# Two query blocks per round in the local attention of a four-layer fp32 kernel

## The reference

```
o = for each 128-query block i, each head h:
    s = q_i k[i-1..i] * scale + (-slope_h * distance, or -1e30 outside the 128-token window)
    m = max(max(s), sink_h);  p = exp(s - m)
    denom = sum(p) + exp(sink_h - m)
    o = (p / denom) v[i-1..i]
x = x + o @ w_out          # q, k are RMS-normed per head first
```

## Time and profile before

| | |
|---|---|
| median of 3 runs | 2162.7 us (2161.97 to 2165.08) |
| profiled execution: time, span | 2161.92 us, 2159.9 us |
| busy in the span | PE 2033.6 (94%), DVE 1127.4 (52%), ACT 796.0 (37%), POOL 136.7 (6%) |
| granted TensorE clock, mean | 0.972 of full |
| local attention stage with its fills | about 665 to 785 us from the span's start |

### The profile page before, as it was taken

The page is one execution under the profiler, slowest core; times in us unless marked ns, Lnnn a source line. Parts: engine busy times, 40 slices in busy tenths (PEclk is TensorE's granted clock), DMA queues, the critical chain, the costliest instruction groups (busy, mean ns, idle before and its releaser), DMA issues. The chain is left out here.

```text
span 2159.9 us, 25160 instructions
## 1 busy us (share of the span) xinstructions
PE 2033.6 (94%) x9068; PEld 1575.3 (73%) x9068; DVE 1127.4 (52%) x1730; ACT 796.0 (37%) x1243; POOL 136.7 (6%) x115
## 2 busy tenths in 40 slices
PE   7967999999999999999999898799989999999999
PEld 5834788888776667888877676588845577888887
DVE  4367456445446756653563765833334536553553
ACT  3145334223335644432342343411145534431341
POOL 0020200000021010000001002200021110000000
PEclk9978999999999999999999999899979999999999
DMA  5200232232221112223222231132200112223222
GB/s 188 95 4 1 78 116 88 88 108 90 82 100 60 40 59 78 97 88 107 98 68 98 78 100 64 54 117 97 87 15 30 44 61 78 96 93 106 94 75 100
DMA packets 30523, 173.85 MB, mean 80 GB/s; under 512 B 3392, under 2 KB 3520, under 8 KB 15472
## 3 DMA queue, kind: packets, MB, share of 16 engines
q1 hardware_dynamic: 30304, 172.66, 23.2%
q10 hardware_dynamic: 144, 0.21, 0.0%
HBM read 170.66 MB, written 2.20 MB: 80 GB/s over the span
## 5 line engine op out<-in xcount | busy, mean ns | idle before, releaser
L539 PE MATMUL banks<-xn_hi,w_hi 128*128 128x512 f32 x1672 | 659.3, 394 | 32.4 <-ACT xn_hi L1047 16.6
L539 PE MATMUL banks<-xn_hi,w_lo 128*128 128x512 f32 x1672 | 654.8, 392 | 0.0
L539 PE MATMUL banks<-xn_lo,w_hi 128*128 128x512 f32 x1672 | 649.0, 392 | 1.1 <-DVEq L1473 1.1
L994 ACT ACTIVATE w_hi<-raw 128x2048 fp32r<-128x2048 f32 (+2 forms) x156 | 271.7, 1742 | 396.1 <-PE banks L539 392.2
L1391 DVE TENSOR_TENSOR w_lo<-raw,w_hi 128x2048 fp32r<-128x2048 f32 (+3 forms) x162 | 339.9, 2098 | 130.7 <-ACT w_hi L994 109.6
L539 PEld LDWEIGHTS banks<-xn_hi,w_hi 128*128 128x128 f32 x1672 | 316.7, 189 | 107.7 <-issue 24.2
L539 PEld LDWEIGHTS banks<-xn_lo,w_hi 128*128 128x128 f32 x1672 | 315.9, 189 | 70.1 <-DVEq L1473 3.4
L539 PEld LDWEIGHTS banks<-xn_hi,w_lo 128*128 128x128 f32 x1672 | 317.0, 190 | 66.4 <-issue 0.2
L1488 DVE SCALAR_TENSOR_TENSOR tmp<-banks,par,tmp 128x511 f32<-128x511 f32 x132 | 98.4, 745 | 269.4 <-ACT tmp L1072 269.4
L1072 ACT ACTIVATE tmp<-banks,par 128x512 f32<-128x512 f32 x132 | 95.6, 775 | 357.3 <-PE banks L539 357.3
L539 PE MATMUL banks<-hid_hi,w_hi 128*128 128x512 f32 x528 | 207.3, 393 | 3.1 <-DVE w_lo L1391 3.1
(11 more groups left out here) (222 smaller groups left out, 2033.5 us busy)
## 6 DMA issues: line engine op xcount, KB each, us to landing
raw<-weights SPq DMA_DIRECT2D x117, 1024.0 KB, 4.8
raw<-weights SPq DMA_DIRECT2D x24, 768.0 KB, 4.2
raw<-weights SPq DMA_DIRECT2D x24, 640.0 KB, 3.7
att<-scratch SPq DMA_DIRECT2D x32, 256.0 KB, 3.1
x<-xt SPq DMA_DIRECT2D x4, 512.0 KB, 5.8
out<-x SPq DMA_DIRECT2D x4, 512.0 KB, 4.0
raw<-weights SPq DMA_DIRECT2D x2, 512.0 KB, 3.4
con<-consts SPq DMA_DIRECT2D x1, 864.0 KB, 12.6
```

Of the source, the lines that this page charges most:

```text
L539: return pe.matmul(psum[:, 2 * p + m, :], w[:, at_:at_ + P], chunk(x_part, k), start=start, stop=stop)
L994: act.activation(w_hi[:, sl], raw[:, sl], ACT.Identity).then_inc(hi_done, 1)
```

## The change

The loop runs over rounds of two steps, g = 0, 2, ... 34. TensorE does the scores of two steps, the fills of two, the turns of the two steps before, and the values of the two before those. ScalarE and VectorE wait for both steps of a round (`g | 1`) before they read a bank, since two steps now share each bank of scores and of transposes, 256 columns each (`c_half`). `c_prob` becomes eight tiles of 257 columns, `c_slot` halves of four chunks, and the bias tiles move. ScalarE's order is `high` at g % 4 == 0, exps of two steps, copies of two steps, `norm_job` at g % 4 == 2, and `hi_piece`. VectorE's is `finish` of two, `maxima` of two, `output` and both `alibi` at g % 4 == 0, `evacuate` of units done in the round before, `lo_piece`, and `scaled` at g % 4 == 2. TensorE's `norm_job` stands at g % 4 == 0, between turns and values. No arithmetic is added or removed.

```diff
         def c_slot(m, g):
-            return att[:, (12 + 2 * (g % 2) + m) * T:(13 + 2 * (g % 2) + m) * T]
+            return chunk(att, 12 + 2 * (g // 2 % 2) + m, 256 * (g % 2), 256 * (g % 2) + 256)
         def c_prob(m, g):
-            return chunk(att, 8 + 2 * (g % 2) + m)
+            at_ = 7 * T + 257 * (2 * (g % 4) + m)
+            return att[:, at_:at_ + 257]
+        def c_half(m, bank, g, w):
+            return psum[:, bank + m, 256 * (g % 2):256 * (g % 2) + w]
...
                 def scores(g):
-                    if g:
-                        pe.wait_ge(c_max, 2 * g)
+                    if g >= 2:
+                        pe.wait_ge(c_max, 2 * (g - g % 2))
...
                 def turn(g):
-                        if g:
-                            pe.wait_ge(c_copied, 2 * g - 1 + m)
+                        if g >= 2:
+                            pe.wait_ge(c_copied, 2 * (g - g % 2) - 1 + m)
...
-                for g in range(C_STEPS + 2):
+                for g in range(0, C_STEPS + 4, 2):
                     if g < C_STEPS:
                         scores(g)
-                    fill(g)
-                    if 1 <= g <= C_STEPS:
+                        scores(g + 1)
+                    if g < C_STEPS + 2:
+                        fill(g)
+                        fill(g + 1)
+                    if 2 <= g <= C_STEPS:
+                        turn(g - 2)
                         turn(g - 1)
-                    if g >= 2:
-                        values(g - 2)
-                    if g % 4 == 1 and g // 4 + 1 < C_PAIRS:
+                    if g % 4 == 0 and g // 4 + 1 < C_PAIRS:
                         norm_job(2 + g // 4 + 1)
+                    if g >= 4:
+                        values(g - 4)
+                        values(g - 3)
...
                 def copy(g):
-                        act.wait_ge(c_pt, 2 * g + m + 1)
+                        act.wait_ge(c_pt, 2 * (g | 1) + m + 1)
...
-                for g in range(C_STEPS + 2):
-                    if g % 4 == 2 and g > 4:
-                        high(g // 4 - 1)
+                for g in range(0, C_STEPS + 4, 2):
+                    if g % 4 == 0 and g > 4:
+                        high(g // 4 - 2)
                     if g < C_STEPS:
                         exps(g)
-                    if 1 <= g <= C_STEPS:
+                        exps(g + 1)
+                    if 2 <= g <= C_STEPS:
+                        copy(g - 2)
                         copy(g - 1)
                     if g % 4 == 2 and g // 4 + 1 < C_PAIRS:
                         norm_job(2 + g // 4 + 1)
                     for s, g0, n in C_FILL:
-                        if g0 <= g < g0 + 2:
-                            hi_piece(s + 1, g - g0, 2)
+                        for q in range(2):
+                            if g <= g0 + q < g + 2:
+                                hi_piece(s + 1, q, 2)
...
                 def maxima(g):
-                    if g >= 2:
-                        dve.wait_ge(c_pt, 2 * g - 2)
+                    if g >= 4:
+                        dve.wait_ge(c_pt, 2 * g - 6)
                     for m in range(2):
-                        dve.wait_ge(c_scored, 2 * g + m + 1)
+                        dve.wait_ge(c_scored, 2 * (g | 1) + m + 1)
...
-                for g in range(C_STEPS + 2):
-                    if 1 <= g <= C_STEPS:
+                for g in range(0, C_STEPS + 4, 2):
+                    if 2 <= g <= C_STEPS:
+                        finish(g - 2)
                         finish(g - 1)
                     if g % 4 == 0 and 0 < g < C_STEPS:
                         sink_columns(g // 4)
                     if g < C_STEPS:
                         maxima(g)
-                    if g % 4 == 2 and g > 4:
-                        output(g // 4 - 1)
-                    if g % 4 < 2 and g // 4 + 1 < C_PAIRS:
-                        alibi(g // 4 + 1, g % 4)
+                        maxima(g + 1)
+                    if g % 4 == 0 and g > 4:
+                        output(g // 4 - 2)
+                    if g % 4 == 0 and g // 4 + 1 < C_PAIRS:
+                        alibi(g // 4 + 1, 0)
+                        alibi(g // 4 + 1, 1)
                     for s, m, done in C_UNIT_STEPS:
-                        if done == g - 1 and done >= 0 and (s, m) != (q + 1, 0):
+                        if g - 2 <= done < g and done >= 0 and (s, m) != (q + 1, 0):
                             evacuate(s, m)
                     for s, g0, n in C_FILL:
-                        if g0 + 1 <= g < g0 + 3:
-                            lo_piece(s + 1, g - g0 - 1, 2)
-                    if g % 4 == 3 and g // 4 + 1 < C_PAIRS:
+                        for part in range(2):
+                            if g <= g0 + 1 + part < g + 2:
+                                lo_piece(s + 1, part, 2)
+                    if g % 4 == 2 and g // 4 + 1 < C_PAIRS:
                         scaled(2 + g // 4 + 1)
```

More of the change, by code:

```diff
@@ L312, in c_slot @@
         def c_slot(m, g):
-            return att[:, (12 + 2 * (g % 2) + m) * T:(13 + 2 * (g % 2) + m) * T]
+            return chunk(att, 12 + 2 * (g // 2 % 2) + m, 256 * (g % 2), 256 * (g % 2) + 256)
         def c_prob(m, g):
-            return chunk(att, 8 + 2 * (g % 2) + m)
+            at_ = 7 * T + 257 * (2 * (g % 4) + m)
+            return att[:, at_:at_ + 257]
+        def c_half(m, bank, g, w):
+            return psum[:, bank + m, 256 * (g % 2):256 * (g % 2) + w]
+        c_bias = [chunk(att, 5), chunk(att, 6)]
         def c_width(g):
@@ L864, in scores @@
                         h = 64 * m
-                        pe.matmul(psum[:, 4 + m, 0:w], qn[it % 2][h:h + 64, i * P:(i + 1) * P], kn[it // 4][h:h + 64, lo:lo + w],
+                        pe.matmul(c_half(m, 4, g, w), qn[it % 2][h:h + 64, i * P:(i + 1) * P], kn[it // 4][h:h + 64, lo:lo + w],
                                   start=True, stop=True).then_inc(c_scored, 1)
@@ L871, in turn @@
                         pe.wait_ge(c_fin, 2 * g + m + 1)
-                        if g:
-                            pe.wait_ge(c_copied, 2 * g - 1 + m)
+                        if g >= 2:
+                            pe.wait_ge(c_copied, 2 * (g - g % 2) - 1 + m)
                         for j in range(w // P):
-                            last = pe.transpose(psum[:, 6 + m, j * P:(j + 1) * P], c_prob(m, g)[:, 256 - w + j * P:256 - w + (j + 1) * P], ident)
+                            last = pe.transpose(c_half(m, 6, g, w)[:, j * P:(j + 1) * P], c_prob(m, g)[:, 256 - w + j * P:256 - w + (j + 1) * P], ident)
                         last.then_inc(c_pt, 1)
@@ L1216, in copy @@
                     for m in range(2):
-                        act.wait_ge(c_pt, 2 * g + m + 1)
-                        if m == 0 and g >= 2:
-                            act.wait_ge(c_pv, g - 1)
-                        act.activation(c_slot(m, g)[:, 0:w], psum[:, 6 + m, 0:w], ACT.Identity).then_inc(c_copied, 1)
+                        act.wait_ge(c_pt, 2 * (g | 1) + m + 1)
+                        if m == 0 and g >= 4:
+                            act.wait_ge(c_pv, g - 3)
+                        act.activation(c_slot(m, g)[:, 0:w], c_half(m, 6, g, w), ACT.Identity).then_inc(c_copied, 1)
                 def high(it):
@@ L1676, in alibi @@
                 def alibi(it, m):
-                    me.mark(dve.tensor_scalar(bias[it % 2][:, 256 * m:256 * m + 256], ccol("window", 0, 256),
+                    me.mark(dve.tensor_scalar(c_bias[it % 2][:, 256 * m:256 * m + 256], ccol("window", 0, 256),
                                               ccol("c_slope", 2 * it + m), None, ALU.mult))
                 def sink_columns(it):
-                    at_ = att[:, 8 * T:12 * T].rearrange("p (a b t) -> p a b t", a=2, b=2)[:, :, :, 256:257]
-                    of = neg_sink[:, 2 * it:2 * it + 2].rearrange("p (o b t) -> p o b t", o=1, t=1).to_broadcast([P, 2, 2, 1])
+                    at_ = att[:, 7 * T:7 * T + 8 * 257].rearrange("p (a b t) -> p a b t", a=4, b=2)[:, :, :, 256:257]
+                    of = neg_sink[:, 2 * it:2 * it + 2].rearrange("p (o b t) -> p o b t", o=1, t=1).to_broadcast([P, 4, 2, 1])
                     me.mark(dve.tensor_copy(at_, of))
@@ L1689, in maxima @@
                         me.wait()
-                    if g >= 2:
-                        dve.wait_ge(c_pt, 2 * g - 2)
+                    if g >= 4:
+                        dve.wait_ge(c_pt, 2 * g - 6)
                     for m in range(2):
                         n = 2 * (g % 4) + m
-                        dve.wait_ge(c_scored, 2 * g + m + 1)
+                        dve.wait_ge(c_scored, 2 * (g | 1) + m + 1)
                         dve.tensor_tensor_reduce(
-                            out=c_prob(m, g)[:, 256 - w:256], in0=psum[:, 4 + m, 0:w],
-                            in1=bias[it % 2][:, 256 * m + 256 - w:256 * m + 256], scale=-1.0,
+                            out=c_prob(m, g)[:, 256 - w:256], in0=c_half(m, 4, g, w),
```

(19 more changed lines are left out.)

## The result

| | before | after |
|---|---|---|
| median, 4 runs each | 2162.8 us | 2197.4 us (2196.8 to 2198.7) |
| ratio, 95% interval | | 1.0159 (1.0141 to 1.0177) |
| span of the profiled execution | 2159.9 us | 2196.2 us |
| PE busy in the span | 2033.6 | 2041.6 (93%) |

The changed kernel is 34.6 us slower; forecast were 29 us. Two executions among all runs of this document that took far longer than the others of their kernel (4127.7 us of the kernel before, 2914.8 us of the version "with one order mended") are left out of the comparisons. The lines have moved: scores are now L872, fills L825, turns L882, values L897, the norm job L861, `scaled` L1688, `evacuate` L1675 and L1679, `lo_piece` L1664, `hi_piece` L1201.

The account below looks back on a forecast made before the run. TensorE, busy 94% of the span, was taken to bound the kernel. Steps 0 to 27 at +23.8 and the rest at -1.3 made +22.5; with +7 for clock, 2161.9 became 2191.4, stated as 2191.5 us, range 2168 to 2207.

Parts of the forecast that it names:

- rival 1: Stalls in the attention stage as the forecast summed them: 2180 to 2203 us, chance 70%.
- its signs: Scores and fills released late, granted clock under 0.9 in 740 to 800, stage about 150; wrong if idle under 10 us.
- The norm chain: Round B's norm job stands behind four exponentials and copies: next scores at 8.0, TensorE idle 2.1 us in seven rounds.
- the sum: Attention stage, round by round at full clock: steps 0 to 27 take 124.8 us against 101.0, the rest 17.3 against 18.7.
- The slab halves: Rounds 4, 12, 20: both `lo_piece` behind second `hi_piece`, next scores at 9.4, four steps 16.2 us; round 2 ends at 10.4.
- The unit banks: Fills wait for later evacuations and output: rounds 20, 22, 24, 26 take 9.8, 12.35, 10.7, 13.6 us.
- Switches saved: TensorE switches between kinds of work once per round instead of twice: 0.34 us saved each two steps, 5.4 at most.
- the scores save nothing: On TensorE, neighbouring scores cost what separate ones do: 0.32 us to the second head, 0.31 to the fill.
- The clock: Low TensorE clock after six gaps (rounds 2, 6, 14, 22, 24, end of 26), 1.2 us each: +7; gaps near 2 free.
- Only the norm chain costs: Bank and slab waits hide behind the norm job's lateness: 2164 us, up to 2172 with clock loss, chance 10%.
- Faster: ScalarE's norm job not behind copies in time, logarithm by 3.6 in round B, TensorE sets the pace: 2149 us, chance 6%.
- The losses feed each other: Every gap halves TensorE's clock and late copies push later rounds: 11 gaps x 1.5 + 30, above 2203 us, chance 11%.

Follow-up runs that it names:

- with one order mended: Kernel before, with VectorE's `scaled` moved ahead of `lo_piece`: 2160.3 us, ratio 0.998.
- The three single mends: Changed kernel with one edit each: norm job at head of round B, 2175.5 us; evacuations and output first, 2184.0; `hi_piece` ahead of copies, 2181.1.
- the kernel mended twice: Mended kernel plus round 2's `lo_piece` first, evacuation ahead of output, round 20's evacuation ahead of slab halves: 2150.5 us, run again 2145.3.
- the other two mends: Changed kernel with evacuations and output at the head of VectorE's round, 2184.0 us; separately with `hi_piece` ahead of the copies, 2181.1 us.
- the mended kernel: Changed kernel with norm job, evacuations and output at their heads, `hi_piece` ahead of copies, `scaled` ahead of `lo_piece`: 2155.1 us, ratio 0.9953.
- the version with useless matmuls elsewhere: Changed kernel with useless matmuls in TensorE's idle time before the scores of rounds 4, 8, 16 and 28: 2194.2 us, ratio 1.0138.
- the late-norm version: Kernel before, single steps, with ScalarE's norm job one step later (g % 4 == 3): 2186.0 us, ratio 1.0097.

## Why the prediction was right, and where it was off

- **Direction and size.** 2191.5 forecast, 2197.4 measured, inside 2168 to 2207. This is rival 1, with a clock loss at about twice its price. Of its signs, TensorE's idle time before the scores was 21.5 us (10 was the bound), the clock granted from 740 to 800 was 0.85, and the stage took 153.0 us. No wait of TensorE in the stage was for a transfer, which the sum had at nothing.
- **The norm chain.** Right in place and size: clean B rounds (10, 18) took 7.8 us against 8.0, with a wait of 1.97 before round 12's scores, and round 6's chain came within 0.3 us at each link. Moving the norm job won 21.9 us, and putting its lateness into the kernel before lost 23.3.
- **The slab halves.** Right in rounds 2, 6 and 14 (10.35, 9.6, 9.6 against 10.4, 9.4, 9.4). Undoing them alone won 16.3.
- **The unit banks.** Right: fills waited for L1679 and L1727 in rounds 20 to 26; undoing it won 13.4. The three single mends add to 51.6 us, while all together, with `scaled` moved as well, gave 42.3. That they share the low clock that each takes away, and round 22, is likely, but was not separated.
- **Switches saved.** The mechanism was right, the size half of it. I had 0.34 us a round of two steps; four steps cost 12.07 us on TensorE in clean rounds (6.34 and 5.73, in the kernel mended twice), against 13.4, so 0.67 a round. The step that failed is "the scores save nothing". I read 0.32 to the second head and 0.31 to the fill as the price of each call; they are the price of entering and of leaving. The four score products of a B round start 0.32, 0.22 and 0.21 apart, and with 0.31 to the fill they take 1.06 us, not 1.26. The rest is in A rounds: turns 0.87 instead of 0.97, and the norm job between them and the values 0.96 instead of 1.06 (round 12). My price of twelve fills, 2.88, did not follow from its own terms (0.34 + 11 x 0.236 = 2.94); they took 2.85. The Trainium skill (TensorE: Matmul & The Clock Gate, Part 3: Packing small matmuls) has small matmuls on different row groups run at the same time, which by my working was worth 10 us over the stage. Neighbouring scores saved 0.2 us a round, 3.2 in 16.
- **The clock.** Named, and mis-sized: six spells at 1.2 us made 7. The trace after shows spells in rounds 4, 8, 16, 22, 24, 26 and 28, at 1.5 to 2.9 us in the four that can be compared with a clean round (8.8 by the experiment). For the other three, with a granted clock of 0.88, 0.61 and 0.87, I add 5 or more, which makes some 14, an estimate. I had the gaps near 2 us as free. That held in rounds 12 and 20, but not in round 24 (1.98 us of waiting, then a granted 0.51 from 772 to 780), and by the experiments it was luck.
- **The 6 us that the sum was short.** In the profiled execution 29.5 us were forecast and 36.3 came. Within the stage it was 33.4, 3.9 more. The larger clock loss (some 7 more) less the under-sized saving (0.33 in each of 16 rounds, 5 more) makes about 2 of it. The other 2.9 lie ahead of the stage and behind it, where the sum had nothing and no cause was found.
- **Other rivals.** "Only the norm chain costs" fell by the other two mends. "Faster" fell by the trace: in round 6 the logarithm starts 7.35 us into the round, where the rival needed 3.6. Its price, 2149 with TensorE alone setting the pace, is what the kernel mended twice reaches (2145 to 2150). "The losses feed each other" fell by the rounds, which came one by one near the forecast but for the clock.
- **Open.** The 1.6 us ahead of the stage and 1.3 behind it, which of the shorter waits bring on low clock, and the wide spread of the best kernel's runs (2143.5 to 2165.0, their mean clock between 0.964 and 0.972), stay open.

## What to carry to other kernels

When steps are grouped to save switches on the busiest engine, every job that feeds the next group must be looked at as well: what stood "one step behind" now stands behind a whole group on its engine. For each such job, write down the chain from the group's first instruction to it and compare it with the group's length on the busiest engine; in this kernel, what depended on nothing in the group did best at its head. The grouping was worth about 10 us and its orders cost about 45. The waits of the busiest engine in the traces of the changed and of the mended kernel, each followed back to what stood ahead of its releaser, pointed at the mends.

## What the runs showed of the hardware

- A wait of 2 us can be followed by the lower clock of TensorE, or not. After 1.97 us the changed kernel's round 12 ran at a granted 1.00; after 1.98 it ran at 0.79 in the version with useless matmuls elsewhere. In the late-norm version five of six waits of 2.0 to 2.3 us were followed by low clock (0.63 to 0.66 over the step). I had taken 2.37 us as safe; that is one case.
- An fp32 product on 64 rows costs about half of one on 128 rows. The useless matmuls (128 rows, 256 columns) took 5.01 us for eleven, 0.46 each; the score products of 64 rows and 256 columns start 0.21 apart when they stand together:

```profile
789.93 5.01 PE L936 MATMUL banks<-con 128*128 128x256 f32 x22
```

- VectorE's scaling takes longer while GpSimd works. In the mended kernel two `finish` scalings took 1.43 us beside GpSimd's square (L507), and 0.62 just after it. It was so in all five places of the stage where the two met; every other pair of this size took 0.61 or 0.62:

```profile
705.35 1.04 POOL L507 TENSOR_TENSOR tn<-big 128x512 f32<-128x512 f32 x1 [11.56 <-DVE big L1675]
705.38 1.43 DVE L1723 TENSOR_SCALAR att<-att,small 128x256 f32<-128x256 f32 x2
...
706.91 0.62 DVE L1723 TENSOR_SCALAR att<-att,small 128x256 f32<-128x256 f32 x2
```
